# The opening of a one-core hybrid attention and MoE layer: paired scale and shift sums in a ring of pieces, a position table by one small write and a flip, parameters loaded later

## The chip, the cores and the metric

The kernel runs on 1 core of one Trainium2 chip. The metric is the device time of one execution in microseconds, the median of several executions of the same program.

## What is computed

One layer over a residual stream x of 256 tokens with 2048 features, and one conditioning vector c. Cut to what matters here:

```python
ada = silu(c) @ w_ada + b_ada                       # w_ada (2048, 6*2048), f32
sh_m, sc_m, gt_m, sh_f, sc_f, gt_f = split(ada, 6)
h = rms_norm(x, g_pre_mix) * (1 + sc_m) + sh_m
proj = h @ w_in                                     # w_in (2048, 6160)
qa, ka, va, qb, kb, vb, rb, zb = split(proj)
bias = rel_bias[t5_bucket(kpos - qpos)]             # 8 heads, 256 x 256
oa = rms_norm(diff_attention(qa, ka, va, bias)) * g_sub_a
log_a = log_sigmoid(zb @ w_alpha + b_alpha) / 16    # zb has 16 columns
ob = rms_norm(gla(qb, kb, vb, log_a)) * silu(rb)
x = x + gt_m * rms_norm(concat(oa, ob) @ w_out, g_post_mix)
h = rms_norm(x, g_pre_ffn) * (1 + sc_f) + sh_f
x = x + gt_f * rms_norm(hier_moe(h), g_post_ffn)    # 32 experts, 3 * 4 MiB each
```

All of it is f32. The six vectors of `ada` are called m = 0 to 5 here: 0 is the shift and 1 the scale of the mixer.

## The kernel before

Every engine runs its own instruction list, written by hand, and waits on semaphores. Nothing is reordered by a tool. The list `SCHED` gives the common order of the part after the opening: 34 slots, each with one half of a projection unit on TensorE (PE; 16 matmuls of 128x256 or 8 of 128x512), and beside it pieces of other work: `ada` n (one of 64 row blocks, 128x2048, of m = 2 to 5), `att` j (attention), `mod` m (the sum over partitions of a finished m), `alpha` 0 to 2 (the decay gates of the linear attention).

**The opening.** Nothing can be projected before m = 0 and m = 1 are known, since h needs them. `w_ada` is laid with 16 of its rows on each partition, so that VectorE (DVE) forms sum over k of `w_ada[k] * silu(c)[k]` in 16 steps per tile (`early(j, m)`, L819 and L821), and PE then adds up the 128 partitions with one matmul of one column for each 128 features (`early_sums`, L500). To overlap this with the projection, the 16 feature blocks are taken in five `STAGES` of 2, 4, 4, 4 and 2 blocks. For each stage SyncE's queue (SP) loads scale and shift of `w_ada` apart, in two halves each (L395), and the rows of `w_in` for seven units of 256 output columns (`early_w`, L400). ScalarE (ACT) makes the stage's part of h (L1194 to L1199), and PE adds the stage's contribution to seven PSUM banks (`early_unit`, L510: 56 matmuls of 128x256 in a stage of four blocks, 28 in one of two). PE does the partition sums of stage j+1 ahead of the last two units of stage j. SP waits for `early_done` (DVE is through with a buffer) or `stage_ps` (PE is through with a stage) before it loads into a buffer again.

**Position table.** PE makes one row of 384 bias values for each of 8 heads (L524, inside stage 0), ACT copies it to SBUF, GpSimd's queue (POOL) writes it 128 times over to DRAM (`skew`, L1376, 8 heads x 128 x 384) and after the opening reads it back with a shifted start for each partition (L1379).

**Parameters.** POOL's queue issues 16 small loads at the start (`params`, L1368), and ACT's queue loads c, the constants, x, and the gate's weights.

**x.** ACT squares x, POOL takes the inverse root, ACT scales x (L1184), and PE transposes it with 32 identity matmuls (L488).

**Sums of m = 2, 3, 4.** When the 16 blocks of an m are accumulated (L861), PE sums the partitions with 16 matmuls of one column (`mod_sums`, L539), and DVE adds the bias (`take_mod`, L865).

**Gate projection.** `alpha` 0 forms the 16 columns of zb with 16 matmuls of 128x256 into 16 partitions (L554).

Of the kernel before, what the change touches and what calls it, by code (L numbers as in the profile page):

```python
# [50 lines left out]
C_ID, C_LT, C_SUF, C_ONE, C_IOTA, C_THR, C_NH, C_HALF, C_BKT = 0, 128, 256, 384, 512, 544, 554, 558, 560  # L51
# [41 lines left out]
def shape_constants():  # L93
# [10 lines left out]
    c[:, C_HALF + 1] = p >= CHUNK  # L104
    rel = np.arange(REL) - (S - 1)
# [40 lines left out]
def loads():  # L146

    out = [(4 * i + 5.9, ("unit", i + 2)) for i in range(8)] + [(SLOTS + 2 * i + 1.9, ("unit", i + 10)) for i in range(2)]
    out += [(max(ada_slot(n - 4) + 0.5, 1.9), ("ada", n)) for n in range(4, 64)]
    return [("unit", 0), ("ada", 0), ("ada", 1), ("unit", 1), ("ada", 2), ("ada", 3)] + [item for _, item in sorted(out)]  # L150

def build(nc, a, out):
# [4 lines left out]
    with ctx:  # L158
# [25 lines left out]
        cums = sb("cums", [1, NE + 1], i32)  # L184
        rel = sb("rel", [P, TT, 2])
# [14 lines left out]
        junk1 = s4[:, 0:D]  # L200

# [63 lines left out]
        def slab(t, lo, n, c):  # L265
# [18 lines left out]
        skew = dram("skew", [A_HEADS, P, SKEW])  # L284
# [1148 lines left out]
```

## Time and profile before

| | |
|---|---|
| median of 3 runs | 1620.8 us (1619.26 to 1621.72) |
| the profiled execution, its own time | 1621.67 us |
| its span, first to last instruction | 1619.9 us |
| PE busy | 1263.6 us (78%) |
| DVE busy | 706.4 us (44%) |
| DMA, mean over the span | 360 GB/s |
| mean granted TensorE clock | 0.891 |

The profile page comes from one execution. Its span is 1.8 us under that execution's own time. A share of busy time is an average over stages with different limits, so the program is read stage by stage: which engine is busy in a stretch, and what ended the last wait in it.
### The profile page before, as it was taken

The page shows a single profiled execution, that of the slowest core. Times are in us where ns is not written, and L with a number is a line of the kernel's source. Part 1 is how long each engine was busy: PE and PEld are TensorE (multiplying, and loading weights), DVE is VectorE, ACT ScalarE, POOL GpSimd, SP SyncE. Part 2 cuts the span into 40 slices and gives each one's busy share as a digit, 9 for nine tenths or more (in the row PEclk, how much of TensorE's full clock was granted, in tenths as well). Part 3 has the DMA queues.
Part 4 walks back from the last instruction along what each step waited for, and adds up shares of the span by engine and source line. Part 5 has one row for each costly group of instructions (what it writes and reads, how often), then busy time and mean ns, then how long its engine had stood idle before and what let it go on. Part 6 is the DMA issues. An engine that isn't in the chain of part 4 may idle for free.

```text
span 1619.9 us, 22071 instructions
## 1 busy us (share of the span) xinstructions
PE 1263.6 (78%) x9205; PEld 637.7 (39%) x9206; DVE 706.4 (44%) x1005; ACT 169.7 (10%) x429; POOL 37.4 (2%) x57
## 2 busy tenths in 40 slices
PE   2639999999999998867667577576675779799755
PEld 2528854575445446323222232232232324244222
DVE  4557326575465543442423324224233244444425
ACT  3101121122101002000000000000000000000001
POOL 3000000000000000100000000000000000000001
PEclk9778999999999999888879888889788889999977
DMA  9989769678765988699999999999999997888994
GB/s 299 317 297 372 278 233 355 256 302 322 291 253 208 383 320 344 267 428 433 424 425 433 424 425 435 421 434 422 425 434 422 425 434 334 359 349 357 430 428 206
DMA packets 93629, 583.18 MB, mean 360 GB/s; under 512 B 5304, under 2 KB 15720, under 8 KB 55712
## 3 DMA queue, kind: packets, MB, share of 16 engines
q1 hardware_dynamic: 90352, 571.49, 86.7%
q10 hardware_dynamic: 1584, 8.02, 1.4%
q0 software_dynamic: 1664, 3.28, 1.3%
q8 instruction: 19, 0.31, 0.1%
q14 instruction: 10, 0.08, 0.0%
HBM read 579.08 MB, written 3.69 MB: 360 GB/s over the span
## 4 chain that ended last, share of the span: by engine, by line
PE 53%; DMA 33%; DVE 7%; SPq 4%; issue 1%; ACT 0%; POOL 0%; DVEq 0%; ACTq 0%
DMA stream<-in_w 29%; PE ps L588 12%; PE ps L750 12%; PE ps L671 7%; PE ps L714 5%; PE ps L776 5%; DMA stream<-in_w_ada 4%; PE ps L510 3%; PE ps L585 3%; SPq L395 2%; PE ps L720 2%; DVE wk L821 1%; DVE wk L1120 1%; PE ps L539 1%; DVE wk L1114 1%
## 5 line engine op out<-in xcount | busy, mean ns | idle before, releaser
L750 PE MATMUL ps<-stream,wk 128*32 128x256 f32 x4608 | 311.2, 437 | 238.3 <-DMA stream<-in_w 236.8
L750 PEld LDWEIGHTS ps<-stream,wk 128*32 128x32 f32 x4608 | 177.9, 126 | 385.1 <-issue 316.3
L1077 DVE TENSOR_TENSOR acc<-ps,acc 128x2048 f32<-128x2048 f32 x37 | 84.8, 2291 | 545.2 <-PE ps L720 545.2
L588 PE MATMUL ps<-stream 128*128 128x512 f32 x448 | 198.8, 599 | 0.0
L776 PE MATMUL ps<-stream,wk 128*32 128x512 f32 x1152 | 131.1, 595 | 16.9 <-DVE wk L1124 16.9
L714 PE MATMUL ps<-resid,wr 128*32 128x512 f32 x592 | 133.7, 1032 | 1.9 <-DVE wr L1064 1.9
L588 PEld LDWEIGHTS ps<-stream 128*128 128x128 f32 x448 | 84.5, 193 | 99.9 <-issue 99.7
L671 PE MATMUL ps<-stream 128*128 128x512 f32 x256 | 112.6, 601 | 1.3 <-issue 1.3
L510 PE MATMUL ps<-stream 128*128 128x256 f32 x448 | 107.1, 404 | 1.8 <-ACT stream L1199 1.8
L510 PEld LDWEIGHTS ps<-stream 128*128 128x128 f32 x448 | 91.4, 205 | 15.8 <-issue 1.9
L861 DVE SCALAR_TENSOR_TENSOR acc<-stream,cc,acc 128x2048 f32<-128x2048 f32 x30 | 70.5, 2348 | 35.0 <-DMA stream<-in_w_ada 33.4
L720 PE MATMUL ps<-wk,cst 32*128 32x512 f32 x592 | 84.1, 639 | 1.0 <-ACT wk L1343 1.0
L1077 DVE TENSOR_TENSOR wk<-ps,wk 128x2048 f32<-128x2048 f32 x37 | 84.4, 2282 | 0.0
L671 PEld LDWEIGHTS ps<-stream 128*128 128x128 f32 x256 | 49.2, 193 | 62.5 <-issue 62.5
L1337 ACT ACTIVATE wk<-ps 128x256 f32<-128x256 f32 x36 | 13.8, 384 | 541.2 <-PE ps L750 541.2
L776 PEld LDWEIGHTS ps<-stream,wk 128*32 128x32 f32 x1152 | 35.0, 109 | 88.8 <-issue 88.8
L821 DVE SCALAR_TENSOR_TENSOR wk<-stream,cc,wk 128x512 f32<-128x512 f32 (+1 forms) x75 | 48.4, 645 | 16.0 <-DMA stream<-in_w_ada 13.3
L821 DVE SCALAR_TENSOR_TENSOR acc<-stream,cc,acc 128x512 f32<-128x512 f32 (+1 forms) x75 | 48.4, 645 | 2.7
L714 PEld LDWEIGHTS ps<-resid,wr 128*32 128x32 f32 x592 | 16.7, 118 | 81.2 <-issue 79.2
L500 PE MATMUL ps<-cst,wk 128*128 128x1 f32 x32 | 6.3, 313 | 47.5 <-DVE acc L821 35.6
L1114 DVE COPY wk<-ps 128x512 f32<-128x512 f32 x36 | 24.9, 692 | 41.9 <-PE ps L714 41.9
L585 PE MATMUL ps<-stream 128*128 128x256 f32 x192 | 42.6, 380 | 0.3 <-PE ps L510 0.3
(243 smaller groups left out, 929.8 us busy)
## 6 DMA issues: line engine op xcount, KB each, us to landing
stream<-in_w SPq DMA_DIRECT2D x128, 2048.0 KB, 23.7
stream<-in_w SPq DMA_DIRECT2D x32, 4096.0 KB, 31.3
stream<-in_w_ada SPq DMA_DIRECT2D x72, 1024.0 KB, 6.9
stream<-in_w_in SPq DMA_DIRECT2D x8, 4096.0 KB, 15.3
stream<-in_w_ada SPq DMA_DIRECT2D x12, 2048.0 KB, 20.4
stream<-in_w_out SPq DMA_DIRECT2D x4, 4096.0 KB, 17.1
stream<-in_w_in SPq DMA_DIRECT2D x3, 3584.0 KB, 23.1
stream<-in_w_in SPq DMA_DIRECT2D x2, 1792.0 KB, 14.3
```

The source lines that it names most:

```text
L510: last = nc.tensor.matmul(bank(u, 2, S)[:, part, :], early_w[j][:, k - lo, 256 * u + P * part:256 * u + P * part + P], hT[:, k, :], start= ...
L585: last = nc.tensor.matmul(bank(fill % 2, 2, S)[:, part, :], w[:, k, lo:lo + P], hT[:, k, :], start=(k == 0), stop=(k == KD - 1))
L588: last = nc.tensor.matmul(bank(fill % 2), hT[:, k, P * half:P * half + P], w[:, k, :], start=(k == 0), stop=(k == KD - 1))
L671: last = nc.tensor.matmul(bank(fill % 2), lhs, w[:, k, :], start=(k == 0), stop=(k == KD - 1))
L714: last = nc.tensor.matmul(bank(0)[32 * g:32 * g + 32, :], pick[:, t2, :], rows[:, t2, 4 * g:4 * g + 4, :], start=(t2 == 0), stop=(t2 == TT ...
L720: last = nc.tensor.matmul(ps[:, b0 + g, :], spread[32 * g:32 * g + 32, t2, :], ye[32 * g:32 * g + 32, :], start=True, stop=True)
L750: last = nc.tensor.matmul(bank(1)[32 * g:32 * g + 32, 0:256], xe[:, k, :], a13[g // 2][:, k, 256 * (g % 2):256 * (g % 2) + 256], start=(k ...
L776: last = nc.tensor.matmul(bank(2)[32 * g:32 * g + 32, :], hid[:, k % 2, 32 * (k // 2):32 * (k // 2) + 32], W2v[:, k, 512 * g:512 * g + 512 ...
L821: ins = V.scalar_tensor_tensor(out=out_, in0=w[:, k, :], scalar=cc[:, 2, k:k + 1], in1=out_, op0=ALU.mult, op1=ALU.add)
L861: V.scalar_tensor_tensor(out=acc_m, in0=w, scalar=col, in1=acc_m, op0=ALU.mult, op1=ALU.add).then_inc(ada_done, 1)
L1077: V.tensor_tensor(y4, ps[:, b0:b0 + 4, :], y4, ALU.add).then_inc(ysum_sb, 1)
L1114: V.tensor_copy(xp, bank(0)).then_inc(rows_sb, 1)
```

## The change

Seven edits, most of them in the opening.

1. **Ring of pieces.** The `w_ada` columns of scale and shift for a stage are loaded together, in pieces of 2 MiB (2 in a stage of two blocks, 4 in one of four; 16 in all), each by two transfers of 1 MiB, into a ring of four buffers. SP waits only until DVE is through with the piece that lay there (`piece_done`). DVE handles both m in one instruction (16 steps of 128x1024 a stage instead of 32 of 128x512).
2. **Sums by 32x32 transposes.** DVE transposes the accumulated tile in 32x32 blocks and adds up each block's rows (`tensor_reduce`). PE is left with four matmuls against a 32-column folding matrix (`fold`). This is done for the stages and for m = 2, 3, 4 (`partial`). There the transpose reads with a stride of 16 elements. m = 5 stays as it was.
3. **Position table.** The row is made and written to DRAM once (8x384, `reldram`), after the opening. It is read back with one start for each partition, which gives the table with its partitions in reverse order, and PE turns it over with a 0/1 matrix (`flip`: four matmuls of 128x512 in slot 6, which ACT copies back).
4. **Late parameters.** POOL issues its parameter loads (12 needed first, 12 later) only after the last stage's sums. The router weights go to a staging place and are copied by POOL.
5. **x.** PE multiplies x with a diagonal matrix that holds the inverse root, so ACT's two scaling passes go.
6. **Gate projection.** The 16 matmuls go to four column groups of 32 (k mod 4), padded by zeros, and w_alpha stands four times under itself.
7. **Order.** `alpha` 0, 1, 2 move from slots 0, 2, 4 to 1, 3, 5. Attention starts in slot 7 instead of 6. The first two `ada` loads come after the second projection unit and wait for the end of the last stage.

```diff
 STAGES = [(0, 2), (2, 6), (6, 10), (10, 14), (14, 16)]
-ATT_FROM = 6
+ATT_FROM = 7
+def pieces(j):
+    lo, hi = STAGES[j]
+    n = KD * (hi - lo) // 16
+    before = sum(KD * (b - a) // 16 for a, b in STAGES[:j])
+    return [(before + i, KD // n * i, KD // n * (i + 1)) for i in range(n)]
...
+    c[:, C_FOLD:C_FOLD + 32] = p[:, None] % 32 == np.arange(32)[None, :]
+    c[:, C_FLIP:C_FLIP + P] = np.eye(P)[::-1]
...
+        early_acc, early_turn, diag = view(wk, 0, 2, D), acc[:, 1024:2048], view(acc, 0, TT, P)
...
+        def turn_of(m):
+            return {2: s3[:, 4096:4096 + D], 3: acc[:, :], 4: s4[:, D:2 * D]}[m]
...
         def _(sp):
             for j, (lo, hi) in enumerate(STAGES):
...
+                for c, k0, k1 in pieces(j):
+                    if c >= 4:
+                        sp.wait_ge(piece_done, c - 3)
+                    for m in range(2):
+                        sp.dma_start(piece(j, c)[:, :, m, :], w_ada[:, k0:k1, m, P * lo:P * hi]).then_inc(piece_in[c % 4], 16)
+                if j >= 3:
+                    sp.wait_ge(stage_ps, j - 1)
                 sp.dma_start(early_w[j], w_in[:, lo:hi, 0:256 * EARLY]).then_inc(early_w_in[j], 16)
-            sp.wait_ge(stage_ps, 3)
             sp.dma_start(half_w, w_in[:, :, 256 * EARLY:2048]).then_inc(half_in, 16)
...
             for t in range(TT):
-                pe.wait_ge(xn, t + 1)
+                pe.wait_ge(diag_sb, t + 1)
...
-                        last = nc.tensor.transpose(bank(j, 4, P)[:, k, :], resid[:, t, P * (4 * j + k):P * (4 * j + k) + P], ident)
+                        last = nc.tensor.matmul(bank((4 * t + j) % 7, 4, P)[:, k, :], resid[:, t, P * (4 * j + k):P * (4 * j + k) + P], diag[:, t, :], start=(k == 0), stop=(k == 3))
...
+            def fold(dst, n):
+                for c in range(4):
+                    last = nc.tensor.matmul(dst[32 * c:32 * c + 32, 0:n // 4], cst[:, C_FOLD:C_FOLD + 32], sums[:, c:n:4], start=True, stop=True)
+                return last
...
-                for m in (1, 0):
-                    for k in range(*STAGES[j]):
-                        last = nc.tensor.matmul(bank(7)[:, 16 * m + k:16 * m + k + 1], acc_of(m)[:, P * k:P * k + P], ones[:, 0:1], start=True, stop=True)
-                last.then_inc(early_ps, 1)
+                pe.wait_ge(part_sb, j + 1)
+                fold(bank(7), 8 * (hi - lo)).then_inc(early_ps, 1)
...
                     if item[1] == 0:
+                        pe.wait_ge(par_in, 16 * len(params))
+                        pe.wait_ge(padded, 2)
                         for k in range(KD):
-                            last = nc.tensor.matmul(bank(5)[0:GATE_RANK, 0:S], wzb[:, k, :], hT[:, k, :], start=(k == 0), stop=(k == KD - 1))
+                            last = nc.tensor.matmul(bank(5)[32 * (k % 4):32 * (k % 4) + 32, 0:S], wzb[:, k, :], hT[:, k, :], start=(k < 4), stop=(k >= KD - 4))
...
+                elif kind == "flip":
+                    pe.wait_ge(bias_in, 16)
+                    for j in range(4):
+                        if j == 3:
+                            pe.wait_ge(flip_sb, 1)
+                        nc.tensor.matmul(bank((2, 3, 6)[j % 3]), cst[:, C_FLIP:C_FLIP + P], wk[:, 512 * j:512 * j + 512], start=True, stop=True).then_inc(flip_ps, 1)
...
+            def early(j):
+                lo, hi = STAGES[j]
+                n = P * (hi - lo)
+                out_ = early_acc[:, :, P * lo:P * hi]
+                for c, k0, k1 in pieces(j):
+                    dve.wait_ge(piece_in[c % 4], 32 * (c // 4 + 1))
...
+                turn = early_turn[:, 0:2 * n]
+                V.transpose(turn.rearrange("p (m n) -> p m n", m=2), out_).then_inc(turned, 1)
+                dve.wait_ge(turned, j + 1)
+                V.tensor_reduce(sums[:, 0:n // 16], turn.rearrange("p (b i) -> p b i", i=32), axis=AX.X, op=ALU.add).then_inc(part_sb, 1)
+            def partial(m):
...
+                turn = turn_of(m)
+                V.transpose(turn.rearrange("p (k i) -> p k i", k=KD), acc_of(m).rearrange("p (i k) -> p k i", k=KD)).then_inc(turned, 1)
+                dve.wait_ge(turned, len(STAGES) + m - 1)
+                V.tensor_reduce(sums[:, 0:64], turn.rearrange("p (b i) -> p b i", i=32), axis=AX.X, op=ALU.add).then_inc(part_sb, 1)
...
+            pool.wait_ge(early_ps, len(STAGES))
...
             for dst, src in params:
                 pool.dma_start(dst, src).then_inc(par_in, 16)
...
+            for dst, src in late:
+                pool.dma_start(dst, src).then_inc(late_in, 16)
             pool.wait_ge(relrow_sb, 1)
-            rr = bass.AP(tensor=relrow.tensor, offset=relrow.offset, ap=[relrow.ap[0], [0, P], [1, SKEW]])
-            pool.dma_start(skew[:, :, :], rr).then_inc(skew_out, 16)
...
+            pool.dma_start(reldram[:, :], relrow).then_inc(rel_out, 16)
+            pool.wait_ge(rel_out, 16)
```

**What stands where on PE.** The rows show PE's list at the first two stages and where the slots begin, before:

```order
L500 MATMUL ps<-cst,wk 128x1 x2
L500 MATMUL ps<-cst,acc 128x1 x2
L510 MATMUL ps<-stream 128x256 x20
L524 MATMUL ps<-wk 8x384
L500 MATMUL ps<-cst,wk 128x1 x4
L500 MATMUL ps<-cst,acc 128x1 x4
L510 MATMUL ps<-stream 128x256 x48
...
L585 MATMUL ps<-stream 128x256 x16
L554 MATMUL ps<-stream 16x256 x16
L585 MATMUL ps<-stream 128x256 x16
```

And the same places in the changed program:

```order
L519 MATMUL ps<-sums,cst 32x4 x4
L540 MATMUL ps<-stream 128x256 x20
L519 MATMUL ps<-sums,cst 32x8 x4
L540 MATMUL ps<-stream 128x256 x48
...
L620 MATMUL ps<-stream 128x256 x32
L583 MATMUL ps<-stream 32x256 x16
L623 MATMUL ps<-stream 128x512 x8
L576 MATMUL ps<-wk 8x384
```

The matmul of the position row (L524, now L576) has moved from inside stage 0 to behind slot 2, the gate's 16 matmuls from behind slot 0 to behind slot 1, and the partition sums are four matmuls each.

**What stands where on DVE.** These are DVE's rows around `mod` 2, from the last attention piece ahead of it, before:

```order
L939 TENSOR_SCALAR wk<-wk,st 128x256
L940 SCALAR_TENSOR_TENSOR wk<-wk,st 128x256
L865 TENSOR_TENSOR mod<-ps,bada 128x16
L871 TENSOR_TENSOR mod<-mod,gains 128x16
L859 TENSOR_SCALAR stream<-stream,cc 128x2048
```

and in the changed program:

```order
L999 TENSOR_SCALAR wk<-wk,st 128x128
L1000 SCALAR_TENSOR_TENSOR wk<-wk,st 128x128
L882 STREAM_TRANSPOSE stream<-acc 128x2048
L884 TENSOR_REDUCE sums<-stream 128x64
L912 TENSOR_TENSOR mod<-ps,bada 128x16
L918 TENSOR_TENSOR mod<-mod,gains 128x16
L906 TENSOR_SCALAR stream<-stream,cc 128x2048
```

A transpose and a reduction over 2048 elements a partition now stand between the last attention piece and the moment at which PE can fold, and that attention piece is the one of 128 keys instead of 256, since attention starts a slot later.

## Rows read from the trace of the kernel before

**Rows 1.** Busy time by stage, all engines; the last columns are PE clock, DMA share, GB/s

```profile
0.00:42.50 42.50, 8.80 (x41) 8.37 (x43) 16.96 (x40) 15.46 (x22) 13.03 (x25) 0.90 0.99 303
42.50:95.80 53.30, 38.78 (x154) 32.57 (x154) 23.28 (x34) 4.61 (x14) 1.17 (x1) 0.79 0.86 262
95.80:123.80 28.00, 3.47 (x17) 3.47 (x17) 23.41 (x32) 0.00 (x0) 0.00 (x0) 0.55 1.03 393
153.20:179.90 26.70, 26.70 (x122) 23.36 (x121) 15.54 (x35) 3.76 (x12) 0.00 (x0) 0.94 1.00 350
199.50:524.00 324.50, 323.16 (x1054) 180.39 (x1054) 176.78 (x197) 55.86 (x173) 9.17 (x14) 0.98 0.74 279
640.00:1600.00 960.00, 699.62 (x7256) 289.90 (x7259) 355.92 (x579) 59.85 (x149) 4.18 (x3) 0.87 0.96 405
```

**Rows 2.** Timeline of the opening: start, duration, instruction, idle time before it

```profile
22.24 3.89 ACT L1184 ACTIVATE resid<-resid,st 128x2048 f32<-128x2048 f32 x2
31.03 7.78 DVE L821 SCALAR_TENSOR_TENSOR acc<-stream,cc,acc 128x256 f32<-128x256 f32 x15
42.52 11.27 PE L510 MATMUL ps<-stream 128*128 128x256 f32 x40 [1.79 <-ACT stream L1199]
55.34 1.17 POOL L1376 DMA_DIRECT2D skew<-wk  x1 [32.22 <-ACT wk L1202]
69.80 23.37 PE L510 MATMUL ps<-stream 128*128 128x256 f32 x96
95.77 0.49 DVE L819 TENSOR_SCALAR wk<-stream,cc 128x512 f32<-128x512 f32 x1 [28.96 <-DMA stream<-in_w_ada]
...
153.22 26.08 PE L510 MATMUL ps<-stream 128*128 128x256 f32 x112
179.95 19.24 PE L510 MATMUL ps<-stream 128*128 128x256 f32 x88
```

**Rows 3.** DMA: two windows as in rows 1, then issues to landing, median us

```profile
80.00:92.00 12.00, 12.00 (x58) 10.55 (x57) 0.00 (x0) 0.00 (x0) 0.00 (x0) 1.00 0.49 73
100.00:150.00 50.00, 29.67 (x125) 26.11 (x126) 41.52 (x58) 3.86 (x13) 0.00 (x0) 0.71 1.03 392
...
skew<-wk POOLq DMA_DIRECT2D x1, 1536.0 KB, 37.2
wk<-skew POOLq DMA_DIRECT2D x1, 1024.0 KB, 12.4
wr<-in_w_router_e POOLq DMA_DIRECT2D x1, 256.0 KB, 12.4
```

**Rows 4.** DVE forms: count, busy us, mean ns, idle before

```profile
L821 DVE SCALAR_TENSOR_TENSOR acc<-stream,cc,acc 128x512 f32<-128x512 f32 x45 | 33.8, 752 | 1.6
L861 DVE SCALAR_TENSOR_TENSOR acc<-stream,cc,acc 128x2048 f32<-128x2048 f32 x30 | 70.5, 2348 | 35.0 <-DMA stream<-in_w_ada 33.4
L932 DVE TENSOR_REDUCE st<-wk 128x2 f32<-128x512 f32 x8 | 5.5, 686 | 0.3
L894 DVE TENSOR_REDUCE wk<-wk 128x36 f32<-128x576 f32 x1 | 1.2, 1178 | 0.0
L893 DVE TENSOR_TENSOR wk<-wr,mod 128x576 f32<-128x576 f32 x1 | 0.8, 752 | 0.0
```

**Rows 5.** PE forms of 199 to 524 us, and of the whole span for L750

```profile
L588 PE MATMUL ps<-stream 128*128 128x512 f32 x448 | 198.8, 599 | 0.0
L554 PE MATMUL ps<-stream 128*16 128x256 f32 x32 | 7.1, 379 | 0.0
L750 PE MATMUL ps<-stream,wk 128*32 128x256 f32 x4608 | 311.2, 437 | 238.3 <-DMA stream<-in_w 236.8 <-DVE wk L1097 1.5
```

**Rows 6.** Timeline at the sums of m = 2, 3 and 4, PE and DVE

```profile
299.26 6.88 PE L539 MATMUL ps<-cst,acc 128*128 128x1 f32 x32
306.18 0.17 DVE L865 TENSOR_TENSOR mod<-ps,bada 128x16 f32<-128x16 f32 x1 [10.26 <-PE ps L539]
405.91 0.17 DVE L865 TENSOR_TENSOR mod<-ps,bada 128x16 f32<-128x16 f32 x1 [9.71 <-PE ps L539]
517.78 6.99 PE L539 MATMUL ps<-cst,acc 128*128 128x1 f32 x32
524.81 0.17 DVE L865 TENSOR_TENSOR mod<-ps,bada 128x16 f32<-128x16 f32 x1 [15.73 <-PE ps L539]
```

More of the change, by code:

```diff
@@ L112, in schedule @@
     beside = [[] for _ in range(SLOTS)]
-    beside[0].append(("alpha", 0))
-    beside[2].append(("alpha", 1))
-    beside[4].append(("alpha", 2))
+    beside[1].append(("alpha", 0))
+    beside[2].append(("row",))
+    beside[3] += [("alpha", 1), ("lam",)]
+    beside[5].append(("alpha", 2))
+    beside[6].append(("flip",))
     beside[ada_slot(15) + 1].append(("mod", 2))
@@ L149, in loads @@
     out += [(max(ada_slot(n - 4) + 0.5, 1.9), ("ada", n)) for n in range(4, 64)]
-    return [("unit", 0), ("ada", 0), ("ada", 1), ("unit", 1), ("ada", 2), ("ada", 3)] + [item for _, item in sorted(out)]
+    return [("unit", 0), ("unit", 1), ("ada", 0), ("ada", 1), ("ada", 2), ("ada", 3)] + [item for _, item in sorted(out)]
 def build(nc, a, out):
@@ L826, in _ @@
-            early(0, 1)
+                n = P * (hi - lo)
+                out_ = early_acc[:, :, P * lo:P * hi]
+                for c, k0, k1 in pieces(j):
+                    dve.wait_ge(piece_in[c % 4], 32 * (c // 4 + 1))
+                    for k in range(k0, k1):
+                        w = piece(j, c)[:, k - k0, :, :]
+                        if k == 0:
+                            ins = V.tensor_scalar(out_, w, cc[:, 2, k:k + 1], None, ALU.mult)
+                        else:
+                            ins = V.scalar_tensor_tensor(out=out_, in0=w, scalar=cc[:, 2, k:k + 1], in1=out_, op0=ALU.mult, op1=ALU.add)
+                        if k < k1 - 1:
+                            link(ins)
+                        else:
+                            ins.then_inc(piece_done, 1)
+                            dve.wait_ge(piece_done, c + 1)
@@ L827, in _ @@
+            early(0)
             dve.wait_ge(kp_ps, 1)
@@ L1181, in _ @@
                 act.wait_ge(xsq, t + 1)
+            act.wait_ge(const_in[0], 16)
             for t in range(TT):
                 act.wait_ge(xr, t + 1)
[L1184 removed]
+                A(diag[:, t, :], ident, ACT.Copy, scale=st[:, 2 + t:3 + t]).then_inc(diag_sb, 1)
             for t in range(TT):
@@ L1235, in _ @@
                         A(st[:, 32:48], bank(7)[:, 0:16], ACT.Exp, scale=1.0 / GATE_TAU).then_inc(suf_exp, 1)
+                elif kind == "flip":
+                    for j in range(4):
+                        act.wait_ge(flip_ps, j + 1)
+                        A(wk[:, 512 * j:512 * j + 512], bank((2, 3, 6)[j % 3]), ACT.Copy).then_inc(flip_sb, 1)
                 elif kind == "proj":
@@ L1365, in rms @@
                 return nc.gpsimd.tensor_tensor(dst, dst, cst[:, C_NH:C_NH + n], ALU.pow)
-            for dst, src in params:
-                pool.dma_start(dst, src).then_inc(par_in, 16)
-            pool.wait_ge(const_in, 16)
+            pool.wait_ge(const_in[1], 16)
             for t in range(TT):
```

202 lines of the change are left out of this document (100 added, 102 removed).

## The prediction

> **What bounds the kernel now.** I read the table by stage first. From 199.5 to 524 us PE is busy 323.16 of 324.5 us: there only PE's own work counts, and a us taken from its list is a us won [rows 1]. From 640 to 1600 us the DMA engines carry 405 GB/s at a share of 0.96: the experts' weights set the pace, the change leaves them alone, and their loads are released by PE's and DVE's progress ahead of them. So this part should move as a block with what happens earlier. What stands open is the first 199 us. PE is busy 3.47 of 28 us between 95.8 and 123.8, with its clock at 0.55 [rows 1].
>
> The timeline says why. DVE stands idle for 28.96 us until the scale columns of stage 2 land at 95.8 [rows 2]. In that time the queues are not short of work but of speed: from 80 to 92 us they move 73 GB/s at a DMA share of 0.49, against 392 GB/s at 1.03 from 100 to 150 [rows 3]. The one transfer in flight that is not a weight load is the 128-fold table write from 8 partitions, issued at 55.34 [rows 2]. It needs 37.2 us, which is 92.5 [rows 3], just ahead of the landing. Half of the engines busy and the weights behind them: I take the write as the cause.
>
> By the Trainium skill ("DMA: Bandwidth & Descriptors", "Why a DMA increments its semaphore by 16 and not by 1") a copy runs on the largest number of engines up to 16 that divides both slowest dimensions, so 8 for these 8 rows. The share of 0.49 agrees. The new write has 8 rows too, but 1/128 of the bytes.
>
> **The opening, rebuilt step by step.** Let transfers run at 392 GB/s [rows 3]. A piece of 2 MiB takes 5.35 us, a stage's w_in of 3.5 MiB 9.4 us, one of 1.75 MiB 4.7 us. DVE costs 752 ns for 512 elements and 2348 for 2048 [rows 4], which is 1.04 ns each, so 1.28 us for 1024 and some 1.32 with the gap to the next: 5.3 us for a piece, as fast as it arrives. The reduction costs 686 ns for 512 [rows 4], so 1.2 us for 1024. No row shows a transpose. I take DVE's 1.04 ns an element where it reads contiguously, 1.2 us, so 2.4 for both; twice and four times this are priced among the rivals, and nothing at all would give 1.2 back.
>
> - *Stage 0.* Before, scale and shift were summed one after the other until 38.8 and PE's first projection matmul stood at 42.52 [rows 2]. In the first 42.5 us the mean was 303 GB/s [rows 1]. x and both pieces are 6.7 MB, with less beside them than before, so I put the second piece at 23 us. Then 8 steps (6.3), transpose and reduction (1.4), three tiny operations, fold and ACT's share of h: PE starts at 34. x is ready by then, since ACT's two passes of 3.89 us together are gone [rows 2]. I allow 31 to 38. Five units take 11.3 us as before [rows 2].
> - *Stage 1.* w_in lands at 27.7, four pieces at 49.1. DVE is through 5.3 + 2.4 later, at 56.8. The next 96 records of PE took 23.4 us before, with the same cold start [rows 2]: 57.1 to 80.5.
> - *Stage 2.* w_in 58.5, pieces 79.9, DVE 87.6. PE waits 7 us, then 112 records, 26.1 when warm [rows 2], some 0.6 more here: 114.6.
> - *Stage 3.* w_in 89.3, pieces 110.7, DVE 118.4. PE waits 4 us, ends at 144.8.
> - *Stage 4.* Pieces 130.8, DVE 138.5, no wait. Its w_in waits for PE's stage 2 (126) and lands by 136. PE's last 88 records take 19.24 [rows 2]: 164.4 instead of 199.2. **34.8 us won.**
>
> The ring never holds a load up here: a piece waits for DVE to finish the one four places back, and two or three pieces or a w_in load are still queued when it does. The edits hang together: no pair of scale and shift, no early finish; without the late parameters and without the table write, none of the DMA room.
>
> **After the opening, PE's list.**
> - The gate's 16 matmuls take 7.1 us [rows 5]. In four column groups the nearest row is L750: 4608 records in 311.2 us, 0.0675 each, so 2.2 us for 32 [rows 5]. -4.9.
> - The position row comes out of a wait into the busy part: 384 of 512 columns of a 0.888 us matmul (448 records in 198.8 us) [rows 5]. +0.65. Four flips: +3.55. ACT's copies run beside them.
> - Sums of m = 2, 3, 4: 6.88, 6.88 and 6.99 us leave [rows 6], four small matmuls come, some 0.35 each: -19.7. But PE now waits for DVE's transpose and reduction. The reduction of 2048 is 2.3 us. The transpose reads every 16th element. The nearest strided row is L894, 1178 ns for 576 elements against 752 contiguous (L893) [rows 4]: 0.74 ns more each, so 3.9 us instead of 2.35 for 2048. I take 6.2 us for both, with 4.6 and 10 as ends.
> - DVE's start: it was idle 10.26 and 9.71 us ahead of taking m = 2 and 3 [rows 6], so free at 295.9 and 396.2, 3.4 and 2.8 us ahead of PE's arrival at 299.3 and 399.0. At m = 2 the shorter attention piece makes that 4.3. Waits: 1.9 and 3.4 us, +5.3. At m = 4 it was idle 15.73 us [rows 6], 8.7 ahead of PE: no wait.
>
> Together -4.9 + 0.65 + 3.55 - 19.7 + 5.3 = **-15.1**.
>
> The Trainium skill ("SBUF — State Buffer", "Door 1: The DMA port swizzle") states that crossing to a new 16-byte line at every access pays a penalty. It speaks against this strided transpose, and L894 agrees. Without the penalty the sum would be 3 us lower.
>
> **Hidden at no cost.** The late loads are issued from about 145 to 165 beside projection; PE asks for the first 12 behind slot 1, at some 179. They land in about 12 us under load [rows 3]. The table: row at 190, write, read-back (12.4 us before [rows 3]) at about 207, flip at 222. If that cover is gone, PE waits by as much as they are late. The first two `ada` blocks come 10 us later than before relative to PE, still ahead of the third, which PE's slot 1 releases.
>
> **Sum.** 1621.67 - 34.8 - 15.1 = 1571.8 for an execution like the profiled one. It stood 0.9 above the median, so 1571.
>
> **The rivals.**
> - *A, forecast*, 0.70.
> - *B, the transpose is slow* (four times 1.04 ns for any stride), 0.13. For it speaks that no row shows it. Early ones cost 3.1 us more, once and not per stage, since w_in's 9.4 us let DVE catch up. The later ones: +4.4 at m = 2 and 3 each, +1.9 at m = 4. 1585.
> - *C, the transfers run slower*, 0.07. For it: 350 GB/s between 153 and 180 [rows 1]. The stretch from 23 to 110.7 us grows by 10.5, PE's waits with it: 1582. The Trainium skill ("DMA: Bandwidth & Descriptors", "Bandwidth") puts the HBM limit of a core at about 358 GB/s, which would give this; 392 and 405 in the rows speak against it.
> - *D, the stall at stage 2 isn't the table write's but those columns' own*, 0.05. Then some 20 of its 28.96 us return: 1591. Against it: the share of 0.49 with work queued.
> - *E, slower: the late parameters.* PE stands at the gate until they land, with attention and all behind it. It decides when they land over 50 us after PE asks, at 229, so 80 us after their issue; at 90 us the kernel takes 1631. The table write's 37.2 us [rows 3] is the most that a transfer took here, 12.4 the usual. 0.02.
> - The rest, 0.03, lies on either side of A.
>
> **Range and chances.** A alone covers 1560 (reduction and transpose at 4.6 us, first start at 31, transfers at 405) to 1583 (start at 38, transposes toward 10). The range of 1559 to 1587 takes in B and C and leaves out D, E and a part of the tails. This kernel's measurement can tell 0.2% (3 us) from no change: faster 0.96, same 0.01, slower 0.03.
>
> **What would show it.** Right: no window of the first 160 us under 350 GB/s except the start; DVE's longest wait for weights under 12 us; `stage 4` records of PE ending near 164; waits of 1 to 4 us on DVE at m = 2 and 3, none at m = 4; the gate's matmuls near 2.2 us. Wrong: a transpose of 2048 elements over 6 us, PE waiting for `par_in` or `bias_in`, or the experts' part not moving as a block, which would mean that it is paced by something that I took to follow PE.

## The result: 49 us faster, as forecast

| | before | after |
|---|---|---|
| median | 1620.0 us of 4 runs (1617.6 to 1621.7) | 1570.75 us of 4 runs (1569.0 to 1572.4) |
| ratio of after to before | | 0.970, 95% interval 0.968 to 0.972 |
| profiled execution, its span | 1621.67, 1619.9 us | 1572.4, 1569.9 us |

The kernel before has one more run here than in the table above, at 1617.6 us. The forecast was 1571 us. From the page of after, the engines' busy time:

```profile
PE 1232.9 (79%) x9149; PEld 608.8 (39%) x9150; DVE 717.4 (46%) x941; ACT 169.7 (11%) x433; POOL 41.4 (3%) x67
```

PE's busy time fell by 31 us and the span by 50, so about 19 us of waiting went too. The table by stage of after answers to [rows 1] (columns as there: us, engines, PE clock, DMA share, GB/s):

```profile
0.00:34.00 34.00, 11.47 (x77) 10.83 (x79) 16.48 (x27) 13.09 (x22) 2.90 (x9) 0.96 0.98 356
34.00:60.00 26.00, 13.42 (x52) 10.95 (x52) 20.22 (x16) 2.86 (x11) 0.00 (x0) 0.70 1.04 398
60.00:90.00 30.00, 23.41 (x104) 19.92 (x104) 22.49 (x18) 3.38 (x12) 0.00 (x0) 0.84 1.04 396
90.00:118.00 28.00, 24.54 (x107) 21.01 (x106) 22.49 (x18) 1.28 (x3) 0.00 (x0) 0.93 1.04 395
118.00:145.00 27.00, 27.00 (x120) 23.31 (x120) 13.16 (x18) 3.76 (x12) 0.00 (x0) 0.90 1.03 346
145.00:165.00 20.00, 19.70 (x98) 16.82 (x97) 0.00 (x0) 5.84 (x13) 13.69 (x24) 1.00 1.05 329
...
590.00:1550.00 960.00, 698.91 (x7257) 289.98 (x7260) 356.37 (x580) 60.09 (x149) 4.21 (x3) 0.87 0.96 405
```

The hole of before, with transfers at half rate and DVE idle, is gone: from 34 to 118 us the engines carry 395 to 398 GB/s throughout. The experts' stretch has the PE, DVE and DMA figures of before.

The timeline of after at the opening's landmarks, answering to [rows 2]:

```profile
32.36 11.81 PE L540 MATMUL ps<-stream 128*128 128x256 f32 x40 [1.82 <-ACT stream L1258]
56.76 0.29 PE L519 MATMUL ps<-sums,cst 128*32 128x8 f32 x8 [12.58 <-DVE sums L870]
87.13 0.29 PE L519 MATMUL ps<-sums,cst 128*32 128x8 f32 x8 [6.59 <-DVE sums L870]
118.00 0.29 PE L519 MATMUL ps<-sums,cst 128*32 128x8 f32 x8 [3.46 <-DVE sums L870]
145.26 0.25 PE L519 MATMUL ps<-sums,cst 128*32 128x4 f32 x8
145.44 19.26 PE L540 MATMUL ps<-stream 128*128 128x256 f32 x88
```

PE's waits ahead of the folds of stages 1 to 4 shrink from stage to stage (12.6, 6.6, 3.5, none). The folds of stages 2 and 3 stand 30.4 and 30.9 us behind the one before, as the transfers let them. The fold of stage 2 has 96 records of PE ahead of it (23.6 us) and that of stage 3 has 112 (27.2 us), and the wait is what is left. The last stage has half as many pieces, so its sums are ready before PE is. The last stage ends at 164.7 us, where it ended at 199.2 before [rows 2].

After the opening, the gate, flip and sums on PE in the timeline, and the waits around m = 2 and 3:

```profile
178.99 1.93 PE L583 MATMUL ps<-stream 128*32 128x256 f32 x32
187.91 0.81 PE L576 MATMUL ps<-wk 32*8 32x384 f32 x2
221.44 3.60 PE L604 MATMUL ps<-wk,cst 128*128 128x512 f32 x8
258.04 3.64 DVE L882 STREAM_TRANSPOSE stream<-acc 128x2048 f32<-128x2048 f32 x1
...
264.06 0.26 PE L519 MATMUL ps<-sums,cst 128*32 128x16 f32 x8 [1.49 <-DVE sums L884]
...
353.26 0.75 DVE L1011 TENSOR_SCALAR stream<-ps,gsub 128x512 f32<-128x512 f32 x1
353.92 3.60 DVE L882 STREAM_TRANSPOSE acc<-stream 128x2048 f32<-128x2048 f32 x1
359.90 0.31 PE L519 MATMUL ps<-sums,cst 128*32 128x16 f32 x8 [4.86 <-DVE sums L884]
360.14 1.23 PE L640 MATMUL ps<-stream 64*128 64x256 f32 x4
361.30 1.22 PE L649 MATMUL ps<-stream,wk 128*128 128x128 f32 x4
362.74 8.66 PE L623 MATMUL ps<-stream 128*128 128x512 f32 x16
...
474.74 0.26 PE L519 MATMUL ps<-sums,cst 128*32 128x16 f32 x8
```

The idle time in brackets is what PE paid for the sums' move: 1.49 us at m = 2, 4.86 at m = 3, nothing at m = 4. From 164.7 to the end of m = 4's sums it is 310.3 us, before from 199.2 to 524.8 it was 325.6 (the end of the matmuls at 517.78 in [rows 6] less that of the last row of [rows 2]): -15.3. From there to the span's end it is 1094.9 against 1095.1 us, so the rest moved as a block.

### The profile page after: what moved, and what is told of

Its sections match the earlier page's. It is cut to its first block, busy times and chain, and to the rows that moved or that the text cites. A ratio compares the mean times of both kernels' runs of the same rounds, so it can differ in the third digit from the quotient of the medians.

```text
span 1569.9 us, 21927 instructions
## 1 busy us (share of the span) xinstructions
PE 1232.9 (79%) x9149; PEld 608.8 (39%) x9150; DVE 717.4 (46%) x941; ACT 169.7 (11%) x433; POOL 41.4 (3%) x67
## 4 chain that ended last, share of the span: by engine, by line
PE 51%; DMA 33%; DVE 8%; SPq 5%; issue 2%; ACT 1%; POOL 0%; DVEq 0%; ACTq 0%
DMA stream<-in_w 30%; PE ps L786 12%; PE ps L623 11%; PE ps L707 7%; PE ps L750 5%; PE ps L812 5%; PE ps L540 3%; SPq L421 3%; DMA stream<-in_w_ada 3%; PE ps L620 3%; PE ps L756 2%; DVE wk L859 1%; DVE wk L1180 1%; DVE wk L1174 1%; SPq L480 1%
## 5 line engine op out<-in xcount | busy, mean ns | idle before, releaser
L623 PE MATMUL ps<-stream 128*128 128x512 f32 x448 | 198.9, 598 | 0.0
L750 PE MATMUL ps<-resid,wr 128*32 128x512 f32 x592 | 133.8, 1032 | 1.9 <-DVE wr L1124 1.9
L623 PEld LDWEIGHTS ps<-stream 128*128 128x128 f32 x448 | 84.0, 192 | 100.1 <-issue 100.0
L540 PEld LDWEIGHTS ps<-stream 128*128 128x128 f32 x448 | 92.5, 208 | 16.4 <-issue 1.9
L859 DVE SCALAR_TENSOR_TENSOR wk<-stream,cc,wk 128x1024 f32<-128x1024 f32 (+1 forms) x75 | 80.4, 1072 | 6.5 <-DMA stream<-in_w_ada 3.9
L707 PEld LDWEIGHTS ps<-stream 128*128 128x128 f32 x256 | 48.4, 190 | 63.2 <-issue 61.3
L750 PEld LDWEIGHTS ps<-resid,wr 128*32 128x32 f32 x592 | 16.8, 118 | 81.2 <-issue 79.2
L908 DVE SCALAR_TENSOR_TENSOR wk<-stream,cc,wk 128x2048 f32<-128x2048 f32 x15 | 35.3, 2351 | 10.3 <-DMA stream<-in_w_ada 9.0
L620 PEld LDWEIGHTS ps<-stream 128*128 128x128 f32 x192 | 36.1, 190 | 5.4 <-issue 0.7
## 6 DMA issues: line engine op xcount, KB each, us to landing
stream<-in_w SPq DMA_DIRECT2D x128, 2048.0 KB, 23.6
```

Source lines behind the costliest of these rows:

```text
L540: last = nc.tensor.matmul(bank(u, 2, S)[:, part, :], early_w[j][:, k - lo, 256 * u + P * part:256 * u + P * part + P], hT[:, k, :], start= ...
L620: last = nc.tensor.matmul(bank(fill % 2, 2, S)[:, part, :], w[:, k, lo:lo + P], hT[:, k, :], start=(k == 0), stop=(k == KD - 1))
L623: last = nc.tensor.matmul(bank(fill % 2), hT[:, k, P * half:P * half + P], w[:, k, :], start=(k == 0), stop=(k == KD - 1))
L707: last = nc.tensor.matmul(bank(fill % 2), lhs, w[:, k, :], start=(k == 0), stop=(k == KD - 1))
L750: last = nc.tensor.matmul(bank(0)[32 * g:32 * g + 32, :], pick[:, t2, :], rows[:, t2, 4 * g:4 * g + 4, :], start=(t2 == 0), stop=(t2 == TT ...
L859: ins = V.scalar_tensor_tensor(out=out_, in0=w, scalar=cc[:, 2, k:k + 1], in1=out_, op0=ALU.mult, op1=ALU.add)
```

## The experiments

The kernel before was run beside each set of these, with medians of 1619.2 to 1619.5 us, and after was run twice, with 1570.75 and 1570.68 us. Single executions of one kernel differ by 2 to 6 us, and the interval of a ratio to the kernel before is 4 to 7 us wide. A difference of 2 or 3 us between two variants is therefore near the scatter, and rests on the rows of the profiles as much as on the medians.

**1. Only the table write moved (edit of before).**

```diff
             pool.wait_ge(relrow_sb, 1)
+            pool.wait_ge(early_ps, len(STAGES))
             rr = bass.AP(tensor=relrow.tensor, offset=relrow.offset, ap=[relrow.ap[0], [0, P], [1, SKEW]])
             pool.dma_start(skew[:, :, :], rr).then_inc(skew_out, 16)
             pool.wait_ge(skew_out, 16)
-            pool.wait_ge(early_ps, len(STAGES))
```

> The kernel before with one line more: the 128-fold table write from 8 partitions waits for the end of the opening instead of going out at 55 us. Theory (the write holds the weights of stage 2 up): the two idle stretches of VectorE for weights at stage 2 shrink from 29 us to under 5, scale and shift of stage 2 land at about 70 and 81 us, its sums are ready at 95 instead of 120, and TensorE's last early matmul ends near 174 instead of 199; the kernel takes about 1595 us (-25), so that the table alone carries some 25 of the 34.5 us that the opening won, the ring, the pairing and the rest about 9. Rival (the stall belongs to those columns of the weights or to the queue's own waits): the idle stretch stays near 29 us and the time at 1620.

It took 1597.4 us (ratio 0.987, 0.985 to 0.989), 21.9 less than before: a little under half of the gain from one moved wait. The window of its stage 2, the wait of DVE there, and the write's new price:

```profile
70.00:92.00 22.00, 22.00 (x95) 19.12 (x96) 18.07 (x25) 3.76 (x12) 0.00 (x0) 0.93 1.05 397
...
73.12 0.49 DVE L819 TENSOR_SCALAR wk<-stream,cc 128x512 f32<-128x512 f32 x1 [6.27 <-DMA stream<-in_w_ada]
155.15 19.24 PE L510 MATMUL ps<-stream 128*128 128x256 f32 x88
...
skew<-wk POOLq DMA_DIRECT2D x1, 1536.0 KB, 35.5
```

The wait of 28.96 us [rows 2] is 6.27, a little over the 5 expected, the transfers run at 397 GB/s, and the opening ends at 174.4, which is 24.8 us earlier. The write still takes 35.5 us; it now lies where the weights have time.

**2 and 3. A 1.5 MiB write put back into after, from 8 and from 128 partitions.** Both write the constants to an unused table, once stage 1 is summed; they add work and change no other. The bytes and the rows of 1536 bytes are the same. The edit with 8 partitions (each row 128 times):

```diff
...
             pool.wait_ge(padded, 1)
+            pool.wait_ge(const_in[1], 16)
+            pool.wait_ge(early_ps, 2)
+            c8 = cst[0:A_HEADS, 0:SKEW]
+            rr = bass.AP(tensor=c8.tensor, offset=c8.offset, ap=[c8.ap[0], [0, P], [1, SKEW]])
+            pool.dma_start(skew[:, :, :], rr).then_inc(skew_out, 16)
             pool.wait_ge(early_ps, len(STAGES))
+            pool.wait_ge(skew_out, 16)
```

and what stands in the place of the three middle lines with 128 partitions (each row 8 times):

```diff
+            c128 = cst[:, 0:SKEW]
+            rr = bass.AP(tensor=c128.tensor, offset=c128.offset, ap=[c128.ap[0], [0, A_HEADS], [1, SKEW]])
+            pool.dma_start(bass.AP(tensor=skew[:, :, :].tensor, offset=0, ap=[[A_HEADS * SKEW, P], [SKEW, A_HEADS], [1, SKEW]]), rr).then_inc(skew_out, 16)
```

> The changed kernel with a dummy copy of the old table write added to its opening: 8 partitions of the constants, 384 values each, 128 times over, to DRAM, 1.5 MiB, issued when the sums of stage 1 are done (57 us). Nothing waits for it before the end of the opening. Theory: it takes 30 us or more to land, the pieces of stage 2 come 18 to 25 us later, and the kernel takes 1588 to 1596 us. Rival (the write was harmless, the gain came from the ring and the pairing): within 4 us of 1571.

> As the run with the dummy write from 8 partitions, with the same 1.5 MiB in the same 1024 rows of 1536 bytes, but read from all 128 partitions, 8 rows each. Theory (what costs is that the rows of 8 partitions lie on half of the DMA engines): it lands in under 12 us, all engines share it, and the kernel takes 1572 to 1577 us, about the 4 us that 1.57 MB take at 392 GB/s. Rival (writing that many bytes or rows to DRAM costs by itself): as with 8 partitions, 1588 or more.

From 8 partitions the kernel took 1594.4 us (0.985, 0.983 to 0.987), from 128 partitions 1573.6 (0.972, 0.970 to 0.974): 23.7 and 2.9 us over after. The same window, the write's issue to landing and DVE's wait, first from 8 partitions:

```profile
70.00:92.00 22.00, 9.53 (x45) 8.05 (x43) 0.25 (x1) 0.00 (x0) 0.00 (x0) 0.82 0.63 116
...
skew<-cst POOLq DMA_DIRECT2D x1, 1536.0 KB, 34.4
91.75 5.25 DVE L861 SCALAR_TENSOR_TENSOR wk<-stream,cc,wk 128x1024 f32<-128x1024 f32 x4 [24.26 <-DMA stream<-in_w_ada]
```

then from 128, whose write goes out at 57.9 us and has landed before 70, so that the window in which it is under way comes first:

```profile
58.00:68.00 10.00, 10.00 (x43) 8.60 (x43) 4.61 (x4) 3.02 (x9) 0.91 (x1) 0.91 1.04 402
70.00:92.00 22.00, 10.61 (x54) 9.05 (x53) 17.88 (x14) 0.81 (x5) 0.00 (x0) 0.81 1.04 399
...
skew<-cst POOLq DMA_DIRECT2D x1, 1536.0 KB, 10.7
72.12 5.25 DVE L861 SCALAR_TENSOR_TENSOR wk<-stream,cc,wk 128x1024 f32<-128x1024 f32 x4 [4.37 <-DMA stream<-in_w_ada]
```

So not the bytes do the harm but the shape. In the first, all transfers together move as little as before (116 GB/s at a share of 0.63; the kernel before has 125 at 0.64 in the same window) and DVE has a wait of 24 us again. In the second the engines move 402 GB/s while the write is under way, and it costs no more than its bytes. POOL's queue holds 43.3% of the 16 engines between 70 and 92 us in the first, near 7 of them. By the Trainium skill ("DMA: Bandwidth & Descriptors", "Why a DMA increments its semaphore by 16 and not by 1") 8 rows get 8 engines, and the near 7 that were busy fit that. A second rule of the Trainium skill ("SBUF — State Buffer", "Door 1: The DMA port swizzle") would slow the same write: partitions 0 to 7 reach two of SBUF's 16 ports. These two runs change both at once and don't tell them apart. The rate of the write gives an estimate: 1.57 MB in 34.4 us are 46 GB/s. Of the 402 GB/s that 16 engines carried beside the other write, 8 would carry some 200, and two sixteenths are 50. So the number of engines alone doesn't explain how slow the write was and the two ports would, but no run shows that they are the cause.

**4. Sums of m = 2, 3, 4 back on PE.**

```diff
                 elif kind == "mod":
-                    pe.wait_ge(part_sb, len(STAGES) + m - 1)
-                    fold(mod_bank(m)[:, 16 * m:16 * m + 16], 64).then_inc(mod_ps, 1)
+                    pe.wait_ge(ada_done, 16 * m - 16)
+                    mod_sums(m, range(KD)).then_inc(mod_ps, 1)
...
+                if n == 2 * KD:
+                    dve.wait_ge(mod_ps, 1)
...
-                    partial(item[1])
```

> The changed kernel with the partition sums of m = 2, 3 and 4 back on TensorE (16 matmuls of one column each); the five early stages keep the transposes. Theory: 20.7 us of matmuls come back, 0.8 us of folding and the waits of 1.5 and 4.9 us for VectorE go: +13.6, so 1584 us. Rival (the transposes cost TensorE as much in waits elsewhere, later in the slots): under +8.

1584.7 us (0.979, 0.977 to 0.980): the transposes of m = 2, 3, 4 are worth 13.9 us, 0.5 us from the prediction's sum for them, 19.7 - 5.3 = 14.4. By the rows of after, 19.9 us leave PE and 6.35 us of waiting come, which is 13.6. The added wait keeps DVE from using the accumulator of m = 2 again, for m = 4, before PE has summed it.

**5. DVE handles scale and shift apart, 512 elements an instruction.**

```diff
-                            ins = V.scalar_tensor_tensor(out=out_, in0=w, ...)
+                        for m in (1, 0):
+                            ins = V.scalar_tensor_tensor(out=out_[:, m, :], in0=w[:, m, :], ...)
```

> The changed kernel with scale and shift summed by one VectorE instruction each again (32 steps of 128x512 a stage instead of 16 of 128x1024); ring, pieces and all else stay. Theory: a piece then takes VectorE 6.3 us instead of 5.3, longer than the 5.35 us in which the next lands, so that a stage of four blocks is ready some 3.5 us later. TensorE starts stage 3 that much later, stage 4 is still hidden: +3 to +4 us, 1574 to 1575. Rival (pairing carries most of what the ring won, since VectorE is the pace): +8 us or more, for 3 times 3.5 that add up.

1574.2 us (0.972, 0.970 to 0.973), +3.4. The folds come at 34.3, 61.4, 90.4 and 120.9 us instead of 30.3, 56.8, 87.1 and 118.0: 2.9 to 4.6 us later and not more with each stage. Transfers, not DVE, set the pace from stage to stage; a slower DVE only adds its tail to each.

**6. DVE's sum one slot ahead of PE's fold.** To take away the waits of 1.49 and 4.86 us, DVE's transpose stays where it was and PE's four matmuls, with what takes their result, go one slot later.

```diff
-    beside[ada_slot(15) + 1].append(("mod", 2))
-    beside[ada_slot(31) + 1].append(("mod", 3))
+    beside[ada_slot(15) + 1].append(("part", 2))
+    beside[ada_slot(31) + 1].append(("part", 3))
+    beside[ada_slot(15) + 2].append(("mod", 2))
+    beside[ada_slot(31) + 2].append(("mod", 3))
```

> The changed kernel with TensorE's folding matmuls and VectorE's taking of m = 2 and m = 3 one slot later than the transpose and the reduction, so that VectorE does these while TensorE projects one more half unit. Theory: TensorE's waits of 1.5 and 4.9 us for the reduction go, nothing else changes: -6.3 us, 1564.5. Rival (VectorE is the pace in these slots and is late again behind them, at its attention pieces): -2 us or less.

1568.5 us (0.968, 0.966 to 0.969), 2.2 less than after, where 6.3 were to be had. These 2.2 us are near the scatter (1564.9 to 1569.6 here, 1568.9 to 1572.4 for after); what follows rests on the profiles. In place of after's waits for the sums, 6.3 us in all, PE has these waits for DVE between 165 and 480 us (engine, waits for, us in total, times, longest):

```profile
PE ps L651 <- DVE wk L1012: 2.7, 1, 2.7
...
PE ps L659 <- DVE wk L1005: 0.8, 1, 0.8
```

and where the new wait comes from, in this kernel's timeline:

```profile
270.89 0.17 DVE L914 TENSOR_TENSOR mod<-ps,bada 128x16 f32<-128x16 f32 x1 [1.88 <-PE ps L521]
...
282.18 0.68 PE L651 MATMUL ps<-stream,wk 128*128 128x128 f32 x4 [2.66 <-DVE wk L1012]
```

The waits for the sums are gone and two others have come. The timeline suggests the reason, and experiment 9 tests it: DVE now stands 1.88 us for PE's fold, and the attention piece behind it on DVE (L1012) begins at 281.35 us, 1.2 later than in after, while PE is earlier by the wait that it no longer has. So at 282.18 PE has waited 2.66 us for that piece. The wait went to the other engine and came back. Still the output projection began at 454.5 us instead of 460.0; some of that was lost again when the granted clock read 0.84 from 469 to 480 us, where after has 1.00. Why it fell there stays open.

**7. A part of the parameters early.** The lambda rows and the late list (router weights and gains) are issued at the start, as before the change; the rest stays late. The router weights go straight to their place, as before the change, and not to a staging place (that part of the edit is left out here), so the run changes both the time and the rows of these loads.

```diff
...
+            for dst, src in params[8:]:
+                pool.dma_start(dst, src).then_inc(par_in, 16)
+            for dst, src in late:
+                pool.dma_start(dst, src).then_inc(late_in, 16)
             pool.wait_ge(const_in[1], 16)
```

> The changed kernel with those parameters loaded at the start again whose places are free then: the four lambda rows and all of the second list, the router weights straight to their place in rows of 16 and 128 bytes. The first eight of the first list stay late. Theory: these small rows take DMA time from x and the first two pieces, the first projection matmul moves from 32.4 to 35 or 37 us, the later stages follow by as much since the transfers pace them: +3 to +5 us, 1574 to 1576. Rival (small loads hide beside the large ones): within 1 us.

1578.3 us (0.975, 0.973 to 0.976): +7.6, above what either theory gave it. Its first 20 us and its first piece, then the same two of after:

```profile
0.00:20.00 20.00, 0.34 (x1) 0.19 (x2) 0.80 (x3) 3.50 (x4) 9.81 (x19) 1.00 0.91 238
...
22.99 0.49 DVE L857 TENSOR_SCALAR wk<-stream,cc 128x512 f32<-128x512 f32 x1 [13.90 <-DMA stream<-in_w_ada]
```

```profile
0.00:20.00 20.00, 2.95 (x13) 2.81 (x15) 4.51 (x9) 6.81 (x9) 2.90 (x9) 1.00 0.94 328
...
15.92 0.49 DVE L857 TENSOR_SCALAR wk<-stream,cc 128x512 f32<-128x512 f32 x1 [9.25 <-DMA stream<-in_w_ada]
```

With about 0.5 MB in small rows more, the first 20 us move 238 GB/s instead of 328 at nearly the same share, and everything starts 7.1 us later; the opening ends 6.4 us later. The kernel before, which has all its parameters there, moves 240 GB/s in these 20 us. The engines were busy, with less to show for it. POOL's queue held 18.0% of the 16 engines in these 20 us, which is 3.6 us; at 392 GB/s its bytes would be 1.3. What makes the 7.1 out of 3.6 isn't settled.

**8. Two pieces in flight instead of four.**

```diff
-                    if c >= 4:
-                        sp.wait_ge(piece_done, c - 3)
+                    if c >= 2:
+                        sp.wait_ge(piece_done, c - 1)
```

> The changed kernel with two pieces in flight instead of four: a piece is not issued before VectorE is through with the one two places back. Theory: the queue runs dry between pieces. A pair of pieces then takes a load of 5.35 us, some 2 us until it is seen, and 5.3 us of sums, so about 6.4 us a piece instead of 5.35: a stage of four blocks is ready some 4 us later each time, and the load of w_in no longer stands between the pieces of two stages unused. +8 to +14 us, 1579 to 1585. Rival (depth does not matter, two are enough to keep the engines fed): within 2 us.

1580.8 us (0.976, 0.974 to 0.977), +10.0. Nothing changes up to the first fold at 30.3; the next ones come at 59.9, 93.2 and 126.7, later each time (by 3.1, 6.0 and 8.7 us against after). Its windows of stages 1 and 2:

```profile
35.00:60.00 25.00, 9.15 (x43) 7.47 (x41) 19.20 (x16) 0.00 (x0) 0.00 (x0) 0.70 0.87 330
60.00:93.00 33.00, 23.66 (x104) 20.05 (x103) 22.49 (x18) 3.76 (x12) 0.00 (x0) 0.81 0.99 367
```

This growing lag is not the pattern of experiment 5. Here the queue has too little issued between pieces (330 and 367 GB/s, where after has 398 and 396), and what is lost in one stage is missing in the next.

**9 and 10. The better version, and after again beside it.** As in 6, and what takes the fold's result (DVE's bias and gains, and POOL's write of the vector) goes behind the attention piece of that slot.

```diff
         beside[ATT_FROM + j].append(("att", j))
+    beside[ada_slot(15) + 2].append(("take", 2))
+    beside[ada_slot(31) + 2].append(("take", 3))
...
-                if kind == "mod" and item[1] == 2:
+                if kind == "take" and item[1] == 2:
                     pool.wait_ge(g_sb, 1)
```

> As the run with the late fold, but VectorE (and GpSimd's write of m = 2) takes the folded values of m = 2 and 3 only behind the attention piece of that slot. The late fold had put a wait of 1.9 us for TensorE's fold into VectorE's list, and TensorE then stood 2.7 us two slots later for VectorE's attention piece. Theory (that wait was what came back, and the half clock behind the 4.9 us wait is worth 2.9 us more): no TensorE wait over 1 us between 165 us and the output projection, which begins 8 to 9 us earlier than in the changed kernel (460.0), so 1562 us. Rival (VectorE is simply full in these slots): a wait of 2 us or more stays and the time is 1566 or more.

> The changed kernel once more, unaltered, on the same chip as the run with the late take, so that the two stand side by side: 1569 to 1573 us. Every theory expects this.

1561.8 us (0.965, 0.964 to 0.966) against 1570.7 for after: 8.9 us less, the fastest kernel here. PE's waits of this version between 165 and 480 us, and its window around m = 3:

```profile
PE ps L661 <- DVE wk L1008: 0.8, 1, 0.8
PE ps L653 <- DVE wk L1015: 0.4, 1, 0.4
...
350.00:371.00 21.00, 20.21 (x69) 9.69 (x68) 17.96 (x16) 3.12 (x12) 0.00 (x0) 1.00 0.97 372
```

and the same window of after, run beside it:

```profile
350.00:371.00 21.00, 16.15 (x46) 7.69 (x45) 17.57 (x19) 2.45 (x9) 0.00 (x0) 0.84 0.93 355
```

No wait for the sums is left, these two, 1.2 us of waiting on attention, have come, and around m = 3 PE is at work for 20.2 of 21 us at full clock instead of 16.2 at 0.84. From the end of the opening to the first matmul of the output projection it is 287.6 us here and 295.4 in after beside it: 7.8 us less, of which 5.1 are waits (6.3 gone, 1.2 come), and the rest fits the 3 us or so by which the matmuls behind the wait at m = 3 are shorter. So the waits of 6.35 us cost more than themselves: the rest came back through the clock. The opening of this profiled execution also ended 1.3 us earlier (163.2 against 164.5), with its stage 3 at 26.1 us instead of 27.3; no edit touches it, so that part of a difference between two profiles is scatter.

## Why the prediction was right

**The cause of the stall** was named rightly and is shown by removing it (1) and putting it back (2). Its rival, that the columns' own transfer was late, is out. The amount: 24.8 us of the 34.5 by the write alone, by the end of the opening in the profiles (21.9 by the medians). Undone one at a time in after, pairing costs 3.4, a part of the parameters 7.6 and two of the four buffers 10.0 us. Single undoings need not add up, and these don't. What the diagonal matrix for x and the transposes give in the opening was not tested by itself.

**The opening**, step by step, forecast and measured: first projection matmul 34 and 32.4, folds at 56.8, 87.6, 118.4 and 56.8, 87.1, 118.0, end 164.4 and 164.7. The start was taken 1.6 us too late, within the 31 to 38 allowed, and it had no effect, since from stage 1 the landings decide. PE's waits of 7 and 4 us were 6.6 and 3.5. That the ring never holds a load up is right for four places and wrong for two (8).

**DVE's new work.** Its forms, after (count, busy us, mean ns, idle before), answering to [rows 4]:

```profile
L882 DVE STREAM_TRANSPOSE stream<-acc 128x2048 f32<-128x2048 f32 x2 | 7.3, 3644 | 0.0
L868 DVE STREAM_TRANSPOSE acc<-wk 128x1024 f32<-128x1024 f32 x3 | 3.7, 1246 | 0.1
L868 DVE STREAM_TRANSPOSE acc<-wk 128x512 f32<-128x512 f32 x2 | 1.4, 711 | 0.1
L870 DVE TENSOR_REDUCE sums<-acc 128x32 f32<-128x1024 f32 x3 | 3.7, 1220 | 0.1
```

The unknown price, a transpose, was put at 1.2 us for 1024 elements read in a row and 3.9 for 2048 at stride 16, and is 1.25 and 3.64. From 711 and 1246 ns a transpose in a row costs 1.04 ns an element and some 0.18 us at the start, so 2.3 us for 2048. What the strided one takes beyond that, 1.3 us, I put down to the stride; no run has 2048 elements transposed in a row. L894, a reduction of 576 elements [rows 4], was a good nearest row. Rival B is out: at four times 1.04 ns the strided transpose would have taken over 8 us. The Trainium skill ("SBUF — State Buffer", "Door 1: The DMA port swizzle") speaks of a penalty where each access crosses to a new 16-byte line, and the 1.3 us, 0.65 ns an element, agree with it.

**After the opening** -15.1 was forecast and -15.3 measured, by pieces that miss both ways: gate -5.15 (forecast -4.9), row +0.81 (+0.65), flip +3.60 (+3.55), sums -19.9 (-19.7), waits +6.35 (+5.3); together -14.3, and -1.0 is left, for which the forecast had no term. That the sum came out within 0.2 us is partly luck. The wait at m = 2 was 1.49 for 1.9. The one at m = 3 was mis-sized, 4.86 for 3.4. I had worked it out from DVE's idle time in the order of before, but in the new order the heads' scaling (L1011, 0.75 us) stands right ahead of the transpose on DVE, which gives half of the miss. The rest is that DVE came to the attention piece of that slot 3.3 us behind PE (349.51 against 346.17), where before it was 1.7 (392.38 against 390.73), less what PE's own later arrival gives back. What I had no term for is PE's clock behind that wait: L640, L649 and L623 take 1.23, 1.22 and 8.66 us there, and 0.70, 0.71 and 7.03 in the slot before (timeline of after, 346 to 355 us). With 0.26 more on L657 that is 2.9 us. Before, such a stretch stood behind the one-column sums, at m = 2 and at m = 3. The window behind those of m = 2, before:

```profile
306.00:309.00 3.00, 3.00 (x10) 1.91 (x11) 2.75 (x5) 0.38 (x1) 1.02 (x1) 0.50 0.17 27
```

Summed in the same way (L604, L613, L621 and L588 against the same instructions at full clock), it cost 2.07 us at m = 2 and 1.75 at m = 3. After has one stretch of 2.93 us for these two, and none at m = 2, where PE waits only 1.49 us and L640 and L623 take 0.70 and 7.03 us. The difference, -0.9, is nearly all of the -1.0. So the clock cancelled in the forecast for the most part, and 9 shows it as a cost.

**Hidden work** stayed hidden. POOL's parameter loads, issued from 146.5 to 159.6 us, landed in 5 to 8 us each and not 12. The forecast took the table write's 37.2 us for the longest transfer of before, but a load of `w_ada` behind it took 49.2 us (L395); no load of after's parameters came near either. Behind the opening, the row's write and wait took 6.0 us, and PE stood at neither the gate nor the flip. E is out. The first `ada` block reached DVE 7.5 us behind the end of the opening (172.2 us), where before it was 10.6 ahead of it (188.6), so it came 18 us later relative to PE and not 10; it cost PE nothing.

**What would show it.** "No window of the first 160 us under 350 GB/s" failed: 346 and 329 from 118 on. The waits of PE for DVE were to be 1 to 4 us, and the second was 4.86. The other signs came: the gate's matmuls took 1.93 us, the last stage ended near 164 us, DVE's longest wait for weights in the opening was 9.3 us, and the experts' part moved as a block. Behind the opening DVE stood 33.7 us for its first `ada` block, which is over the 12 us named, but PE had no wait from it. In the two slow windows the DMA share is 1.03 to 1.05, so the engines were not idle, but the packets are smaller. The DMA view of after, from 60 to 118 us and from 118 to 165 us:

```profile
DMA packets 9205, 22.93 MB, mean 395 GB/s; under 512 B 271, under 2 KB 890, under 8 KB 9202
...
DMA packets 10304, 15.91 MB, mean 339 GB/s; under 512 B 561, under 2 KB 6150, under 8 KB 10302
```

Six in ten packets are under 2 KB in the second stretch, one in ten in the first. No run changes the packets alone, so that they are the cause is not shown. PE waited for none of these loads, so it cost nothing; as a general statement on the rate the sentence was wrong. Rival C gave one rate to the whole opening and is out: the stages that matter ran at 395 to 398.

## What to carry to other kernels

A transfer should be judged by how its rows lie over partitions, not by its bytes: 1.5 MiB from 8 partitions cost the kernel 24 us, the same from 128 cost 3. Before moving a sum to another engine, read what stands ahead of it and behind it there in the new order: the wait lands on whoever asks next, and moving it one slot helps only if the other side's follow-up moves too (6 against 9). When a chain is paced by arrivals, a slower consumer costs its tail once, but too few buffers cost more with each stage.

## What the hardware showed that I had not expected

- Behind a wait of 4.9 us on PE the granted clock read 0.50 for 3 us and 0.81 for the 8 after those, though DVE and DMA were at work:

```profile
360.00:363.00 3.00, 3.00 (x19) 2.31 (x20) 2.58 (x4) 0.02 (x1) 0.00 (x0) 0.50 1.05 392
363.00:371.00 8.00, 8.00 (x16) 3.37 (x16) 6.47 (x8) 1.34 (x5) 0.00 (x0) 0.81 0.80 294
```

  These are windows of after. 0.50 is the lower level, 1.2 GHz. In version 6, which has no wait there, the clock reads 1.00 in both. Before, where PE was not idle but ran 6.9 us of one-column matmuls, it reads 0.50 behind them as well (window above). Behind the wait of 1.49 us at m = 2 it reads 1.00 (264 to 275 us).
- About 0.5 MB of small loads at the start delayed everything by 7.1 us (experiment 7).
- The transfers ran at 395 to 405 GB/s for long stretches. The Trainium skill ("DMA: Bandwidth & Descriptors", "Bandwidth") has a limit of about 358 for a core. The Trainium skill ("HBM Reference", "Specifications (TRN2)") says that a core that streams alone gets more, about 425, and the rates of this one-core kernel fit that.
